# A two-block network on one core: the delta-rule inverse formed for 64-token diagonal blocks, and two places for the context's work in each slice of an expert

## The reference, cut to what matters

```python
lower = where(strict, einsum('id,jd->ij', k_beta, k) * decay, 0)
a_mat = eye(CHUNK) + lower
sol   = triangular_solve(a_mat, rhs, lower=True, unit_diagonal=True)
u, w  = sol[..., :dv], sol[..., dv:]
# per chunk
v_new = u - w @ s
o     = q_dec @ s + qk @ v_new
s     = s * g_end + k_dec.T @ v_new
```

## Time and profile before

| | us |
|---|---|
| median of 3 runs (3275.04 to 3290.93) | 3277.28 |
| the profiled execution | 3272.05 |
| its span | 3270.3 |
| TensorE busy in it | 2691.0 (82%) |
| VectorE busy | 972.2 (30%) |
| ScalarE busy | 414.0 (13%) |
| DMA, main queue | 775.62 MB, 60.1% of 16 engines |

### The profile page before, as it was taken

How to read it: one execution, slowest core, us unless ns; L and a number is a source line. 1 busy time by engine, 2 the same in 40 slices (tenths; PEclk the granted TensorE clock), 3 DMA queues, 4 the chain that set the end, 5 groups by cost and what they waited for, 6 DMA issues and landing times. The chain is left out here.

```text
span 3270.3 us, 42263 instructions
## 1 busy us (share of the span) xinstructions
PE 2691.0 (82%) x18791; PEld 1468.6 (45%) x18791; DVE 972.2 (30%) x1961; ACT 414.0 (13%) x806; POOL 85.9 (3%) x93
## 2 busy tenths in 40 slices
PE   7969568988999999898889888774883586969995
PEld 4535133333443435344434322263872585735553
DVE  0237343102223113213313100145635643042222
ACT  1122011101001001112211100111012221000001
POOL 0010000000000000000000000000000110000000
PEclk9978769999999999999999998886995787979998
DMA  5307038998889887976887899750000002339997
GB/s 173 116 30 280 0 145 339 383 386 328 313 333 372 331 339 280 386 319 265 318 344 319 318 412 404 315 188 5 1 20 13 2 3 89 121 144 399 422 422 296
DMA packets 159151, 790.91 MB, mean 242 GB/s; under 512 B 18273, under 2 KB 20585, under 8 KB 111225
## 3 DMA queue, kind: packets, MB, share of 16 engines
q1 hardware_dynamic: 155513, 775.62, 60.1%
q0 software_dynamic: 3456, 12.58, 1.0%
HBM read 776.62 MB, written 11.53 MB: 241 GB/s over the span
## 5 line engine op out<-in xcount | busy, mean ns | idle before, releaser
L2970 PE MATMUL bank<-ring,arena 128*34 128x512 f32 (+1 forms) x3072 | 719.7, 604 | 101.3 <-DMA ring<-in_w_up 75.4
L2970 PEld LDWEIGHTS bank<-ring,arena 128*34 128x34 f32 x3072 | 176.0, 117 | 491.3 <-issue 465.0
L2994 PE MATMUL bank<-ring,arena 128*34 128x512 f32 x1408 | 321.1, 597 | 46.5 <-DMA ring<-in_w_down 45.8
L2994 PEld LDWEIGHTS bank<-ring,arena 128*34 128x34 f32 x1408 | 78.8, 112 | 279.0 <-issue 151.1
L305 PE MATMUL bank<-arena,ring 128*128 128x256 f32 (+1 forms) x688 | 159.1, 395 | 11.3 <-DMA ring<-in_w_in 9.6
L305 PEld LDWEIGHTS bank<-arena,ring 128*128 128x128 f32 x688 | 134.5, 196 | 36.1 <-issue 10.5
L3417 PE MATMUL bank<-ring,arena 128*64 128x256 f32 x992 | 111.3, 379 | 4.6 <-DMA ring<-in_moe_w_up 3.8
L2718 PEld LDWEIGHTS bank<-arena 128*128 128x128 f32 x656 | 81.6, 195 | 62.4 <-issue 57.8
L2870 PEld LDWEIGHTS bank<-arena 64*64 64x64 f32 x2304 | 73.9, 136 | 60.2 <-issue 60.0
L315 PE MATMUL bank<-ring,arena 128*128 128x512 f32 (+1 forms) x224 | 98.8, 596 | 0.0
L2718 PE MATMUL bank<-arena 128*128 128x128 f32 x656 | 96.6, 291 | 0.8 <-DVE arena L1790 0.8
(11 more groups left out here) (627 smaller groups left out, 3222.0 us busy)
## 6 DMA issues: line engine op xcount, KB each, us to landing
ring<-in_w_gate SPq DMA_DIRECT2D x128, 1408.0 KB, 9.8
ring<-in_w_up SPq DMA_DIRECT2D x128, 1408.0 KB, 12.6
ring<-in_w_down SPq DMA_DIRECT2D x176, 1024.0 KB, 8.9
ring<-in_w_in SPq DMA_DIRECT2D x46, 1024.0 KB, 6.4
ring<-in_moe_w_down SPq DMA_DIRECT2D x33, 1024.0 KB, 15.7
ring<-in_moe_w_gate SPq DMA_DIRECT2D x31, 1024.0 KB, 13.9
ring<-in_moe_w_up SPq DMA_DIRECT2D x31, 1024.0 KB, 16.9
ring<-in_ada_w SPq DMA_DIRECT2D x24, 1024.0 KB, 7.0
```

The source lines that it names most:

```text
L2970: last = mm(ps[c][row:row + CAP, 0:n], xsT[:, e, k, :], w[:, at:at + n], start=k == 0, stop=k == KT - 1)
L2994: last = mm(ps[6][row:row + CAP, :], hidT[:, 2 * j + f, :], w[:, f, half * BANK:(half + 1) * BANK], start=j + f == 0, stop=j == FT // 2 - ...
```

## The change

**Inverse.** It is formed for the two 64-token diagonal blocks of a chunk alone, so the level 64 goes (`LEVELS` = 2 to 32). Blocks of both directions stand in one tile of 128 x 512: the partition half is the block, the columns are direction, head, column. A group is now 16 products of 64 x 64 (`blocks_of`), and one VectorE operation serves both directions. The product with the right side becomes a block solve in three steps (`solved`): the first half, the other half's right side less the off-diagonal block times the first result, the second half. Masks come from `join7`, and `join` and its two loads go. In the latent part the two operations on the right side move behind the update of X within the first level.

**Places.** A slice has two places, at c = 3 and at its end (the last slice one), 15 in an expert; VectorE and ScalarE advance once at the slice's start instead of twice. The chunks start at place 50, RWKV's inputs at 108, its steps at 132, up to 232 of 240.

**Small.** The 48 small transposes of the modulation go to one bank instead of two, with a wait between; the wait for `join7` moves ahead of the chunks.

```diff
-        LEVELS = (2, 4, 8, 16, 32, 64)
+        LEVELS = (2, 4, 8, 16, 32)
-        def slot_number(e, k, third=2):
-            return 23 * e + 3 * k + third
+        def slot_number(e, k, end=1):
+            return 15 * e + 2 * k + end
-        AT_RK, AT_RV, AT_LO, AT_STEPS = (7, 5), (8, 0), (8, 4), slot_number(8, 6)
+        AT_RK, AT_RV, AT_LO, AT_STEPS = (7, 1), (8, 0), (8, 4), slot_number(8, 6, 0)
...
-                    if c in (2, 4):
+                    if c == 3:
                         next(context, None)
...
@@ context, TensorE
+                    def blocks_of(lhs, rhs):
+                        for d in range(2):
+                            for h in range(4):
+                                for hb in range(2):
+                                    r = half7(hb)
+                                    last = mm(a_both[r, d, h, :], lhs(r, d, h, hb), rhs(r, d, h), start=True, stop=True)
+                        return last
+                    def solved(step):
+                        for h in range(4):
+                            for d in range(2):
+                                first, second = half7(d), half7(1 - d)
+                                if step == 1:
+                                    last = mm(a_wide[second, h, :], lT_c[d][first, h, C7 * (1 - d):C7 * (2 - d)], vnew_c[d][first, h, :], start=True, stop=True)
+                                else:
+                                    r = second if step else first
+                                    last = mm(a_wide[r, h, :], xT_c[r, d, h, :], rhs_c[d][r, h, :], start=True, stop=True)
+                        return last
...
                     for i, s in enumerate(LEVELS):
-                        for d in range(2):
-                            token = for_dve(heads(bank_a, lambda h: lT_c[d][:, h, :], lambda h: xm_c[d][:, h, :]))
+                        token = for_dve(blocks_of(lambda r, d, h, hb: lT_c[d][r, h, C7 * hb:C7 * (hb + 1)], lambda r, d, h: xm_c[r, d, h, :]))
...
-                    for d in range(2):
-                        token = for_act(heads(bank_a, lambda h: xT_c[d][:, h, :], lambda h: rhs_c[d][:, h, :]))
+                    token = for_act(solved(0))
+                    yield from until(at[0] + 1)
+                    copied_by_act(token)
+                    token = for_dve(solved(1))
+                    yield from until(at[0] + 1)
+                    read_by_dve(token)
+                    token = for_act(solved(2))
...
@@ latent tokens, TensorE
+                for i, s in enumerate(LEVELS):
+                    if i == 0:
+                        pe.wait_ge(x_copied, due(pe, x_copied))
+                    else:
+                        pe.wait_ge(step_read, due(pe, step_read))
+                    blocks_of(0, lambda r, d, h, hb: lT[d][r, h, C7 * hb:C7 * (hb + 1)], lambda r, d, h: xm[r, d, h, :]).then_inc(step_filled, up(step_filled))
+                    pe.wait_ge(step_read, due(pe, step_read, 2 if i else 1))
+                    if s != LEVELS[-1]:
+                        blocks_of(1, lambda r, d, h, hb: xT_[r, d, h, :], lambda r, d, h: p1[r, d, h, :]).then_inc(step_filled, up(step_filled))
+                    blocks_of(4, lambda r, d, h, hb: p1[r, d, h, :], lambda r, d, h: xT_[r, d, h, :]).then_inc(step_filled, up(step_filled))
+                pe.wait_ge(step_read, due(pe, step_read))
+                pe.wait_ge(rhs_ready, due(pe, rhs_ready, 2))
+                solved(5, 0).then_inc(new_filled, up(new_filled))
+                pe.wait_ge(new_copied, due(pe, new_copied))
+                solved(6, 1).then_inc(step_filled, up(step_filled))
+                pe.wait_ge(rhs_ready, due(pe, rhs_ready))
+                solved(5, 2).then_inc(new_filled, up(new_filled))
+                pe.wait_ge(new_copied, due(pe, new_copied))
...
@@ latent tokens, VectorE
+                    TT(p1, in_bank(0), join7[:, :, i + 1].unsqueeze(2).to_broadcast([P, 2, 4, C7]), ALU.mult).then_inc(step_read, up(step_read))
+                    for x, b in ((xm, 1), (xT_, 4)) if s != LEVELS[-1] else ((xT_, 4),):
+                        dve.wait_ge(step_filled, due(dve, step_filled))
+                        TT(x, x, in_bank(b), ALU.subtract).then_inc(step_read, up(step_read))
...
@@ latent tokens, ScalarE
+                for step in range(2):
+                    act.wait_ge(new_filled, due(act, new_filled))
+                    for d in range(2):
+                        r = half7(d if step == 0 else 1 - d)
+                        last = ACTV(vnew[d][r], bank4(5)[r], ACT.Copy)
+                    last.then_inc(new_copied, up(new_copied))
```

More of the change, by code:

```diff
@@ L1206, in _ @@
                 for k in range(KT):
-                    next(context, None)
                     next(context, None)
@@ L1805, in context_dve @@
                             yield from until(at[0] + 1)
[L1806 to L1809, removed]
+                    yield from until(at[0] + 1)
+                    bank_filled()
+                    for d in range(2):
+                        r = half7(1 - d)
+                        last = TT(rhs_c[d][r], rhs_c[d][r], a_wide[r], ALU.subtract)
@@ L1810, in context_dve @@
+                    bank_read(last)
                     yield from until(at[0] + 2)
@@ L3109, in _, with blocks_of, solved @@
                     last.then_inc(g_products, up(g_products))
+                def blocks_of(bank, lhs, rhs):
+                    for d in range(2):
+                        for h in range(4):
+                            for hb in range(2):
+                                r = half7(hb)
+                                last = mm(in_bank(bank)[r, d, h, :], lhs(r, d, h, hb), rhs(r, d, h), start=True, stop=True)
+                    return last
+                def solved(bank, step):
+                    for h in range(4):
+                        for d in range(2):
+                            first, second = half7(d), half7(1 - d)
+                            if step == 1:
+                                last = mm(bank4(bank)[second, h, :], lT[d][first, h, C7 * (1 - d):C7 * (2 - d)], vnew[d][first, h, :], start=True, stop=True)
+                            else:
+                                r = second if step else first
+                                last = mm(bank4(bank)[r, h, :], xT_[r, d, h, :], rhs[d][r, h, :], start=True, stop=True)
+                    return last
+                pe.wait_ge(x_ready2, due(pe, x_ready2, 2))
+                blocks_of(2, lambda r, d, h, hb: xT_[r, d, h, :], lambda r, d, h: ident[r, r]).then_inc(x_turned, up(x_turned))
                 for d in range(2):
                     c = ORDER[d][p]
-                    pe.wait_ge(x_ready2, due(pe, x_ready2))
-                    for h in range(4):
-                        nc.tensor.transpose(ps[4 * d + 2][:, h * P:(h + 1) * P], xT_[d][:, h, :], ident)
                     for h in range(4):
@@ L3136, in _ @@
-                for d in range(2):
-                    pe.wait_ge(step_read, due(pe, step_read))
-                    pe.wait_ge(rhs_ready, due(pe, rhs_ready))
-                    for h in range(4):
-                        last = mm(ps[4 * d][:, h * P:(h + 1) * P], xT_[d][:, h, :], rhs[d][:, h, :], start=True, stop=True)
-                    last.then_inc(new_filled, up(new_filled))
-                for d in range(2):
-                    pe.wait_ge(new_copied, due(pe, new_copied))
+                    last.then_inc(step_filled, up(step_filled))
```

174 lines of the change are left out of this document (78 added, 96 removed).

## The result

The changed kernel takes 3184.20 us as the median of 4 runs (3169.67 to 3184.71), the kernel before 3276.16 (3269.34 to 3290.93) in the same comparison; the ratio is 0.9703 with a 95% interval of 0.9660 to 0.9746. The forecast was 3189. The profiled execution took 3184.11 us, with a span of 3182.3 against 3270.3: 88.0 less, which is the sum that the forecast reached; part of that closeness is luck, as said further down.

A forecast was written before the change was run, and what follows sets the result against it. TensorE bounds experts with context, weights' DMA those without, and the TensorE-VectorE chain the latent delta rule. Experts -74 and latent -14 sum to -88: 3272.05 becomes 3184 profiled, forecast 3189 us; own range 3168 to 3212, 8 in 10 3154 to 3230.

The forecast's parts named there:

- The bound: Experts: slices with context are set by TensorE, those without by weights; floors 6.80 us a slice, 83.7 an expert.
- TensorE's work: Context products in the experts: 22.8 us saved a pass, 45 taken for two, bounds 38 and 52.
- The rival of one bank: Groups of sixteen run singly because both halves write one PSUM bank: 3244 us, chance 0.03.
- Idle time: Experts: 17 us filled, 11 and 3 off VectorE's waits L1957 and L1738, against 5 and 2 us charged.
- the step from -69 to -74: Experts: terms sum to -69, adding up slices instead gives -83 us; -74 was taken.
- the filling of experts 13 to 15: Some 33 RWKV steps move from experts 9 to 12 into idle time of 13 to 15: 17 us saved.
- the charge of 7 for more waiting and fuller rings: Experts: 5 us for slightly more idle time over ten experts, 2 us for weight pieces delayed by context pieces holding buffers.
- The signs named in advance: Experts 4 and 6 about 91 to 94 us, 13 and 14 95 to 100; latent level 3.8, tail 7.7.
- The latent part: Latent delta rule, per pass: levels save 15.5 us, level 0 costs 0.8, solves 6.7; two passes -16, with clock -14.
- the allowance for the clock: Latent delta rule's tail: TensorE idles, a group at 1.2 GHz costs 1 us more, one allowed per pass.
- DMA: Rival in experts 3 to 15: weights arrive later, 3 us more each, +39, giving 3228 us; chance 0.15.
- waits go too: Rival in the experts: waits L1957 and L1738 vanish, slices follow their sum, another 33 us, giving 3156; chance 0.14.

The follow-up runs named there:

- the experiment with three places: Changed kernel with the three places in a slice of the kernel before, so the shorter inverse alone: 3232.55 us, ratio 0.9872.
- the two later runs that have the change's experts: Changed kernel with six idle products behind each latent solve, 3174.71 us; changed kernel with the right side's operations moved into the second and third levels, 3178.76 us.
- the run with the long inverse: Kernel before with two places in a slice (15 in an expert) and its own inverse kept: 3279.15 us, ratio 1.0016.
- the idle products for the tail: Changed kernel with six idle 128 x 128 products behind each of the latent part's three solves: 3174.71 us, ratio 0.9696.
- the run with the right side moved: Changed kernel with the right side's four VectorE operations moved from behind the first level into the second and third: 3178.76 us, ratio 0.9699.
- the second step behind the down product: Changed kernel with three places inside the down product, and slice 0's place moved to be a second one behind it: 3125.46 us, ratio 0.9533.

## Why the prediction was right, step by step

**The bound** was read rightly: slices with context are TensorE's, those without the weights'. That the experiment with three places left expert 6 at 84.40 us, against the 83.7 of the earlier trace rows, shows the floor of an expert. The floor of a slice, 6.80, was read wrongly: k = 7 of expert 4 took 6.00.

**TensorE's work**: 45 us taken, 45.0 measured by groups and 44.9 by windows. The terms came out close: a group 1.20 instead of 1.16, a solve 1.10 instead of 1.18. The agreement to a tenth is luck, though. In the two later runs that have the change's experts TensorE's busy time fell by 52 to 55 us; and a group's busy time runs on into the product behind it, so that, counted from each product's start to the next one's, the inverse's groups fell by 41.7.

That two products in the two partition halves run side by side though both write one bank is shown by the trace: in a group (L3144, L3156) the records of the two halves start 6 to 7 ns apart. For products of 128 columns such a pair of records comes every 0.11 us, and so does each single record of the full products in the earlier trace rows, of which every product has two: two products for the price of one. The rule of the Trainium skill (TensorEngine Tiling (Array Packing), Restrictions and Gotchas) that row tiles can't access one bank at once does not hold for these pairs, whose outputs lie in different partition halves; the measurement decides. The rival of one bank falls with it.

**Idle time** in the experts fell by 34.2, where the terms added up to 24 and the step from -69 to -74 made it 29 (the sum by slices, -83, on which that step leans, stands without its terms and can't be redone). By wait: L1957's 9.8 less (11 taken), L1738's 6.2 less (3), L1843's 3 less (not priced), that for w_up 13.1 less, that for w_down 1.7 more. The term that was mis-sized is the filling of experts 13 to 15, 17 us: their idle time fell by 8.5, from 39.0 to 30.5. The wait for w_up there did fall by 12.2, but VectorE's (L1961, 5.9 instead of 2.0) came with the steps. What made up for it stood elsewhere: the charge of 7 for more waiting and fuller rings didn't come, and L1738 and L1843 gave 6 more than taken. The room that the places alone open was sized rightly, as the run with the long inverse shows (31 us, 28 allowed).

**The signs named in advance.** Expert 4 took 91.5 and expert 6 90.7 us (91 to 94 named), expert 14 94.0 and expert 13 102.3 (95 to 100). Experts 13 to 15 grew by 24.7 us together, just under the 25 that would have counted against the forecast. The latent level's period was 3.94 (3.8) and the tail 9.1 (7.7).

**The two parts of the change need each other.** In the experts the inverse alone gives 25.6 us, the places alone cost 8.2 (little more than the scatter of that stretch), together they give 78.4. The forecast booked the places under the term for experts 13 to 15, and named the eight free places; that they fit only by the shorter inverse it didn't say.

**The latent part** was forecast at -14 and gave -11.3. Pass 1 gave its 7; what was off lies in pass 0. Its levels gave 13.6 instead of 15.5: 1.5 of the difference is that one of them ran partly at 1.2 GHz (its three groups took 4.56 us instead of 3.09), and 0.4 that three of them have a period of 3.94 instead of 3.8. The solve cost 8.0 instead of 6.7, and the products behind it 1.9 more, which the allowance for the clock (1 us a pass) held only in part. That this was the clock is shown by the idle products for the tail, and for the level by the run with the right side moved. Up to the p1 of level 1 the pass came out 0.5 shorter, not 0.8 longer.

**Rivals.** DMA did not take the gain: of experts 3 to 15, eight have 6.6 to 8.0 us of idle time and five 10.5 to 12.3, where seven had over 11 before. The granted clock in experts 1 to 15 stayed at 0.92 to 0.97. What was seen of "waits go too" was the part above. Behind the latent part the span is 2.8 us longer. That is scatter: the run with the places alone, which changes nothing there, took 879.7 for the same stretch where the kernel before took 876.3.

**Luck.** The experts gave 4.4 us more than forecast, the latent part 2.7 less, and the last stretch 2.8 back. That these cancel to 88.0 is chance. What the experiments bear out are the mechanisms: TensorE's work as the bound beside the context, the idle time that the weights leave, and the latent chain of levels and solves.

## What to carry to other kernels

When work is filled into the gaps of another stream, its worth depends on where it is put: look for the stretch in which the filled engine waits for transfers (here the down product, which no place reached) before making the filler cheaper. Halving a triangular inverse and solving by blocks trades long levels for serial steps; it pays at once where other work runs beside, and gives back half where nothing does, the more so as the standing engine's clock falls. Check that a schedule with fewer places still holds all of the steps: a step that spills cost 3.0 us here, one in a gap next to nothing.

## What the runs showed of the hardware

Eight products of 64 x 64 by 128 columns took 1.09 us at the full granted clock and 1.97 at half of it (1.2 GHz), to which it fell in the change behind waits of 0.8, 1.3 and 1.6 us. The same waits do not always do it: in two of the six profiles that have them (the latent part alone, and the second step behind the down product) all three solves stayed at 1.09 in both passes. Six idle products in each wait kept them at 1.09. Two such products in different partition halves, writing one bank, started 6 to 7 ns apart and took 0.22 us of the engine together, as one full product of 128 columns does. A copy or subtraction on 64 partitions by 512 values took about as long (0.60 on ScalarE, 0.69 on VectorE) as one on 128 partitions, so splitting an operation by partitions doubles its cost.
